# Within a slot of the second block's attention stage, TensorE turns an older softmax unit's rows behind the new unit's scores

## What is computed

```python
def dilated_mixer(qkv, qk_gain, slopes):        # 3 groups of 2 heads, each group its own dilation
    s = q . k * scale - slope * distance         # per group, masked
    p, lse = masked_softmax(s, valid)
    ...
    return sum over groups of softmax(lse) * (p @ v)

def nsa_mixer(q, kv, gate_logits, ...):          # 4 heads; compressed, selected and window attention
    ...
    return g[..., 0:1] * o_c + g[..., 1:2] * o_s + g[..., 2:3] * o_w

def stick_breaking_mixer(qkv):                   # 6 heads
    z = q . k * scale
    after = reverse cumulative sum of log_sigmoid(-z), without the own element
    a = where(causal, exp(log_sigmoid(z) + after), 0)
    return a @ v

x = x + concatenate([o_a, o_b, o_c]) @ w_out
```

## Time and profile before

| what | value |
|---|---|
| median of three executions | 2247.91 us |
| the profiled execution's own time | 2248.13 us |
| its span, first to last instruction | 2246.4 us |
| around the span | 1.7 us |
| PE busy, share of the span | 83% |
| DVE, ACT, POOL busy | 59%, 45%, 30% |
| mean granted clock of PE | 0.91 |
| slots 25 to 91 and the last output pieces | about 1568 to 1861 us |

### The profile page before, as it was taken

The page is one execution under the profiler, slowest core; times in us unless marked ns, Lnnn a source line. Parts: engine busy times, 40 slices in busy tenths (PEclk is TensorE's granted clock), DMA queues, the critical chain, the costliest instruction groups (busy, mean ns, idle before and its releaser), DMA issues. The chain is left out here.

```text
span 2246.4 us, 28568 instructions
## 1 busy us (share of the span) xinstructions
PE 1870.6 (83%) x8580; PEld 1453.0 (65%) x8582; DVE 1321.8 (59%) x1608; ACT 1014.4 (45%) x1304; POOL 681.8 (30%) x534
## 2 busy tenths in 40 slices
PE   5787988996640999999999991198989886998999
PEld 2674656775540788888888880166656555887887
DVE  1682644455461899999999982735556654333232
ACT  1322433432101788888888871234455533222221
POOL 0594992000005466666666650001001110000000
PEclk9799999997855999999999995599889998999999
DMA  6744542221102999999999983343211003232222
GB/s 242 180 148 145 144 129 67 62 72 69 63 0 105 357 364 372 363 369 376 371 364 359 357 313 139 129 104 80 63 38 43 11 10 104 94 96 88 97 93 75
DMA packets 168407, 373.53 MB, mean 166 GB/s; under 512 B 40588, under 2 KB 77992, under 8 KB 159880
## 3 DMA queue, kind: packets, MB, share of 16 engines
q1 hardware_dynamic: 148888, 325.45, 42.3%
q0 software_dynamic: 19440, 47.05, 6.5%
HBM read 355.77 MB, written 29.29 MB: 171 GB/s over the span
## 5 line engine op out<-in xcount | busy, mean ns | idle before, releaser
L108 DVE TENSOR_TENSOR exp_parts<-exp_raw,exp_parts 128x2048 fp32r<-128x2048 f32 x192 | 434.9, 2291 | 56.5 <-ACT exp_parts L1683 56.1
L1683 ACT CAST exp_parts<-exp_raw 128x2048 fp32r<-128x2048 f32 x192 | 365.2, 1916 | 93.3 <-DMA exp_raw<-in_w_exp_up 80.1
L102 PE MATMUL ps<-exp_parts,xgT 128*128 128x512 f32 x1536 | 377.7, 401 | 6.6 <-issue 6.3
L102 PEld LDWEIGHTS ps<-exp_parts,xgT 128*128 128x128 f32 x1536 | 286.1, 190 | 77.5 <-issue 11.8
L102 PE MATMUL ps<-exp_parts,exp_hT 128*128 128x512 f32 x768 | 196.4, 405 | 2.1 <-DVE exp_hT L108 2.1
L1576 POOL DMA_INDIRECT xg<-h_rows,row_index x64 | 149.4, 2334 | 112.1 <-issue 106.0
L102 PE MATMUL ps<-h4T,w_up_parts 128*128 128x512 f32 x768 | 176.1, 392 | 8.5 <-DVE w_up_parts L108 8.5
L102 PE MATMUL ps<-w_down_parts,hidden_parts 128*128 128x512 f32 x768 | 176.4, 392 | 7.1 <-DVE w_down_parts L108 7.1
L102 PEld LDWEIGHTS ps<-h4T,w_up_parts 128*128 128x128 f32 x768 | 145.2, 189 | 39.2 <-ACT w_up_parts L144 8.7
L102 PEld LDWEIGHTS ps<-w_down_parts,hidden_parts 128*128 128x128 f32 x768 | 145.6, 190 | 37.9 <-issue 7.5
L102 PE MATMUL ps<-h3T,w_parts 128*128 128x512 f32 (+1 forms) x576 | 153.9, 420 | 14.2 <-DVE w_parts L108 14.2
(11 more groups left out here) (416 smaller groups left out, 3223.8 us busy)
## 6 DMA issues: line engine op xcount, KB each, us to landing
exp_raw<-in_w_exp_gate SPq DMA_DIRECT2D x130, 512.0 KB, 5.9
exp_raw<-in_w_exp_up SPq DMA_DIRECT2D x130, 512.0 KB, 7.8
exp_raw<-in_w_exp_down SPq DMA_DIRECT2D x64, 1024.0 KB, 8.0
w_up_raw<-in_w_up SPq DMA_DIRECT2D x15, 1024.0 KB, 5.2
w_down_raw<-in_w_down SPq DMA_DIRECT2D x15, 1024.0 KB, 5.0
yk<-y_rows SPq DMA_DIRECT2D x8, 1536.0 KB, 16.9
w_raw<-in_w_in SPq DMA_DIRECT2D x42, 256.0 KB, 3.4
gate_cols<-in_w_mod POOLq DMA_DIRECT2D x20, 512.0 KB, 4.4
```

Of the source, the lines that this page charges most:

```text
L102: mm = nc.tensor.matmul(out, left[a], right[b], start=start and i == 0, stop=stop and i == 2)
L108: return nc.vector.tensor_tensor(dst, x, high.bitcast(F32), ALU.subtract)
L1683: nc.scalar.copy(dst, src).then_inc(s_hi[kind], 1)
```

## The change

In each slot PE's program does the turn of unit `k - 30` behind the stick scores, the `follow` entries and the new unit's scores, where it did it first. All instructions, waits, buffers and the programs of the other engines stay as they are.

```diff
             for k in range(SLOTS):
-                if 0 <= k - U0 - LT < UNITS:
-                    soft_turn(k, k - U0 - LT)
                 if k in STICK_SLOT:
                     stick_scores(k, *STICK_SLOT[k][1:])
                 for i in FOLLOWED:
                     if k == FOLLOW_SLOT[i]:
                         follow(k, i)
                 if 0 <= k - U0 < UNITS:
                     soft_scores(k - U0)
+                if 0 <= k - U0 - LT < UNITS:
+                    soft_turn(k, k - U0 - LT)
                 if k in CHUNK_SLOT:
                     project(CHUNK_SLOT.index(k))
```

## The result

| what | before | after |
|---|---|---|
| median of 20 executions each | 2251.41 us (2247.23 to 2261.72) | 2258.46 us (2252.35 to 2270.36) |
| ratio after / before | | 1.0028 [1.0015, 1.0041] |
| the profiled execution: own time, span | 2248.13, 2246.4 us | 2252.35, 2250.6 us |
| start of the span to the stage's first weight load | 1453.1 us | 1454.7 us |
| first weight load to the stage's last addition | 407.1 us | 408.3 us |

The changed kernel is slower: the interval of the ratio lies above 1, though its lower end, 1.0015, is less than the 0.2% that I had called the least that can be told. Its median lies 2 us above the upper end of my range. The table holds two further things. Twenty executions of the kernel before have a median of 2251.4; the three that I started from (2247.91) and the profiled one (2248.13) were at the low end.

The account below looks back on a forecast made before the run. PE was taken as close to the bound with a few waits, ACT's queue beginning with the copy the change delays. Gains -3.0 and losses +5.3 gave +2.3 us on 2248.13, called 2250.3; range 2243.5 to 2256.5.

Parts of the forecast that it names:

- Slot 30: Turn waited 2.81 us; scores of 1.08 fill it, but the stick turn then waits for ACT's copy: gain 0.65.
- Slots 43 to 46: Scores fill slot 43's wait, gain about 1.05; slot 45's stick turn comes 0.88 later, +1.1 in all by slot 46.
- Slots 61 to 65: Late ACT copy delays POOL's operation, DVE's scaling and the bank 4 copy: loss 2.4 us, bounds 0.5 to 3.5.
- Slot 69: Scores fill a wait of 2.23 us; copy and short output product cost some 0.15: gain 0.5.
- Slot 39: ACT's copy moves from 1639.72 to 1640.61 and the delay carries whole to slot 43's wait: loss 0.9 us.
- Slots 76 to 79: Stick copy, POOL, scaling and logarithm each about 0.9 us later; +0.9 stays.
- rival A: Waits in front of turns are simply filled, ACT's queue having slack: -6.4 us, or 2241.5; chance 0.13.
- I leave their number as it is: Low-clock stretches of PE, 2.5 to 3.2 us each, kept at the same count in the forecast.
- slots 40 and 64: Longer PE waits there could pull the clock down, while shorter ones in slots 30 and 43 could keep it up.
- B: Longer PE waits at 1644 and 1764 bring two more slow stretches: +8.0 us, or 2255.9; chance 0.27.
- C: New scores cannot start in the wait, their bank not being free: within 0.2%; chance 0.05.

Follow-up runs that it names:

- eight stages: Norm and mixer stage of the second block eight times, each start delayed by more short ACT copies: old order 3487.26 us, new order 3505.15 us.
- second profile of after: Changed kernel run again unchanged: median 2257.68 us over 12 executions, its profiled stage 415.1 us.
- only the losses' slots moved: Four stages, turn moved only in slots 39, 40, 45, 46, 61 to 65 and 76 to 78: 1796.24 us, +26 against the old order.
- repeated stages: Norm and mixer stage of the second block four times, first block and MLP left out: old order 1770.39 us, new order 1786.41; also run eight times.
- second profile of before: Kernel before run again unchanged: median 2250.74 us over 12 executions, its profiled stage 410.5 us.

## Why the prediction was wrong

I forecast 2250.3 us and "within 0.2%"; it is 2258.5, +0.3%. Put by stretches between maxima, the forecast's terms, the profiled pair, and the mean over eight stages (the two runs with delays):

| slots | forecast | profiled pair | eight stages |
|---|---|---|---|
| 29 to 36 | −0.85 | −2.5 | −2.4 |
| 36 to 40 | +0.9 | +1.7 | +3.7 |
| 40 to 43 | 0 | −0.4 | −0.4 |
| 43 to 52 | 0 (−1.05 + 1.1) | 0.0 | −0.2 |
| 52 to 54 | 0 | −0.2 | +1.0 |
| 54 to 61 | −0.6 | +0.1 | −0.4 |
| 61 to 64 | +2.4 | +2.5 | +1.8 |
| 64 to 73 | −0.5 | −0.7 | −0.7 |
| 73 to 80 | +0.9 | +0.5 | +0.5 |
| 80 to the end | 0 | −0.8 | −0.8 |
| sum | +2.3 | 0.0 | +2.2 |

The maxima that cut the stretches come earlier in their slot by about the turn that was in front of them (0.30 to 0.63 us), in slots 30 to 80; so a single entry, the first and the last above all, is off by that much, and the sum is not. The sum over eight stages is from the profiled executions (3478.21 and 3504.66 us, 26.5 apart, 17.4 of it in these stretches); the one of the old order was 9 us under its median, so that both ways give +2.2 per stage is partly chance.

**The queues were read about right place by place, their sum was not.** *Slot 30:* the wait went from 2.81 to 2.15, with 0.45 of a new wait for ACT: the 0.65 that I took. *Slots 43 to 46:* counted from the turn that ends the long wait, the stick turn of slot 45 came 14.44 us later before (1678.09 − 1663.65) and 14.22 after (1679.79 − 1665.57), −0.22 where I had −1.05 + 0.88 = −0.17. *Slots 61 to 65:* +1.7 by itself; the rows above show the very chain, POOL's operation 2.96 us later against the stick scores of slot 61 (12.20 against 9.24), DVE's scaling stretched to POOL's end, and the wait of 4.65. In the profiled pair 2.5 came of it, since the clock of that stretch was 0.92; in the second profile of after, at 1.00, it was 13.35 − 11.61 = 1.7. *Slot 69:* −0.5 as taken. *Slot 39:* ACT's copy moved by 0.42 us, 0.2 of it after subtracting the shift already there at slot 36, not by 0.9 (with only the losses' slots moved, slots 36 to 40 did take 0.9 more). *Slots 76 to 79:* +0.5, not +0.9, and what I let stand to the end was given back there: −0.8 behind slot 80. Over all of it, take off half of the change in low-clock time (an estimate: a microsecond at 0.50 does half a microsecond's work, if PE is not waiting): of the +2.2 over eight stages 0.3 is left (more if PE waits through some of that time), and the profiled pair, with equal low-clock time, differs by 0.0. By that my gains and losses came near to cancelling, where I had +2.3. Two slips of the text are small beside that: the terms of rival A add up to −6.5, not −6.4, and the projection of 4.76 us that I took for one at the low clock ran at 0.60; one wholly at 0.50 took 5.04.

**The step that failed** is "I leave their number as it is", on the low-clock stretches, by which the clock's term was nothing. From slot 29 to the end the clock stood at 0.50 for 42.2 us per stage in the old order and 46.1 in the new one (mean of eight), by the estimate above up to 1.9 of the 2.2 us; in the second profiles of the two whole kernels it was 44.4 and 54.6, and they differ by 4.5 us there. The two largest entries of the measured means are mostly clock: slots 29 to 36, where the low stretch began later (in the repeated stages slots 28 to 30 were granted 0.76 in the old order and 1.00 in the new one), and slots 36 to 40, where the low-clock time went from 3.8 to 11.0 us. Without the small products of slots 36 and 38 the change costs 0.35 us per stage instead of 4.0. I had looked for new slow stretches behind longer waits only (slots 40 and 64). In the profiled pair there was one, behind the wait of 3.64 in slot 40: 2.04 us for 1.10 of products (in the repeated stages both orders have it). For both of them, the later fall at slot 30 and this one, the Trainium skill (TensorE: Matmul & The Clock Gate, section "What's actually happening"), by which low is the default and recent activity releases the clock, had pointed the right way, and the trace agrees. The costly ones, behind slots 36 and 52, lay where PE had no wait at all, only thin products, and they came, or grew longer, with a shift of about a microsecond in what ran before. I had the first of them on hand, in the row of 4.76 us, and did not ask what stood in front of it. That the cost there hangs on the thin products is shown (+3.9 us in slots 36 to 40 with them, +0.3 with 28 of 32 left out), though part of that may be the room that PE gained; how a shift decides it is not shown.

**The rivals.** B, slower by more low-clock stretches, was nearest: +8.0 against a measured +3.6 to +7. Its place was wrong for the most part: a low stretch behind the wait near 1644 did come in the profile of after, the one near 1764 stands in both, and the decisive ones are behind the small products of slots 36 and 52. A is excluded, since the filled waits (6.5 us) gave no time back. C is excluded by the same row: the scores did run in the waits.

**The base.** The 2248.13 from which I summed was itself 3 us low, in part by clock too: its slots 52 to 54 took 12.95 us at 1.00, the second profile of before 14.57 at 0.88. From 2251.4, the forecast would have been 2253.7, still 5 below, but B's 8.0 from there gives 2259.4, above the measured 2258.5: the range was missed by the base as much as by the clock.

**What stays open.** The repeated stages give +2.2 to +4.0 per stage, the whole kernel +3.6 to +7. All that lies outside the stage took 1839.3 and 1845.7 us in the two profiled executions of before, 1842.4 and 1843.2 in those of after, and whether the changed stage shifts the clock of the MLP behind it was not tried. Nor was it shown why the old order falls into one pattern in each stage and the new one does not.

## What to carry to other kernels

Where an engine's program is a fixed order, look at what stands behind the consumer's entry on its engine. In the repeated stages moving the producer later inside its slot paid only with the consumer moved later too: each of the two moves alone lost (+4.0 and +2.3 us per stage by the medians) and both together gained 2.6. In the whole kernel both together could not be told from no change. When PE is near its bound and the clock has stretches at either level, an edit of a microsecond moves those stretches; price them as a term of their own (here up to some 5 us, with either sign), and look for where the clock can fall behind runs of thin products as well as behind waits. Do not sum from one profiled execution: repeat the stage in one kernel, and take the base from more than three runs.

## What the hardware showed unexpectedly

- Stretches of continuous PE work ran at either level in kernels that differ only in what came several slots earlier: slots 36 to 40 took 25.7 us at a clock of 0.93 and 31.2 at 0.76, with products of the same shapes and the low stretch in slot 36 behind 32 products of 31 columns, without a wait.
- Delaying a stage's start by up to seven short copies on ACT left it as long as before (277.2 to 278.0 us): whether the work and the clock settle to one pattern, or the delays were too short, stays open.
- DVE's scaling of 512 columns took 0.55 us alone and 2.90 beside POOL's operation of 3.44; it began 0.81 behind POOL and ended at 1761.83, 0.27 behind POOL's end at 1761.56. The Trainium skill (SBUF — State Buffer, section "Who interferes with whom") says that operations of this kind can, in one of DVE's modes, take a port that they share with GpSimd, and that the one issued second is then blocked until the first is done; these rows look so in the main. Blocked to the very end it would have ended 0.55 behind POOL and not 0.27, the times of POOL in a profile are rough, and no run here varied the DVE operation to test it.
